# Delta heads: sums of squares as two rounded matmuls of a split square

## The reference, cut to what matters

```python
def l2norm(t):
    return t * lax.rsqrt(jnp.sum(t * t, axis=-1, keepdims=True) + 1e-6)

def gated_deltanet(h, w_in, conv_w, a_log, dt_bias, o_norm_g, w_out):
    qkv, gate, a_raw, b_raw = jnp.split(h @ w_in, ...)
    qkv = jax.nn.silu(causal_dwconv(qkv, conv_w)).astype(f32)
    q, k, v = jnp.split(qkv, [GDN_QK, 2 * GDN_QK], axis=-1)
    q = l2norm(q.reshape(bsz, L, GDN_HEADS, GDN_DK)) * (GDN_DK ** -0.5)
    k = l2norm(k.reshape(bsz, L, GDN_HEADS, GDN_DK))
    ...
    # triangular systems of each chunk, then the recurrence over chunks
    o = rmsnorm(o, o_norm_g) * jax.nn.silu(gate.astype(f32).reshape(...))
    return o.reshape(bsz, L, GDN_V).astype(h.dtype) @ w_out
```

## Time and profile before

| | us |
|---|---|
| median of 3 runs | 3143.57 |
| lowest and highest | 3140.71 and 3145.73 |
| the profiled execution | 3141.96 |
| its span, first to last instruction | 3140.2 |
| PE busy | 3054.4 (97%) |
| DVE busy | 1886.1 (60%) |
| ACT busy | 1110.5 (35%) |
| POOL busy | 598.6 (19%) |

### The profile page before, as it was taken

How to read it: one execution, slowest core, us unless ns; L and a number is a source line. 1 busy time by engine, 2 the same in 40 slices (tenths; PEclk the granted TensorE clock), 3 DMA queues, 4 the chain that set the end, 5 groups by cost and what they waited for, 6 DMA issues and landing times.

```text
span 3140.2 us, 41151 instructions
## 1 busy us (share of the span) xinstructions
PE 3054.4 (97%) x14594; PEld 2491.2 (79%) x14594; DVE 1886.1 (60%) x2257; ACT 1110.5 (35%) x1502; POOL 598.6 (19%) x1031
## 2 busy tenths in 40 slices
PE   8999999999999999998998899999999999989997
PEld 6888888878888888886886788888887788878886
DVE  6545454557677676776337455555555566666666
ACT  4111111245445454454134344444433222222223
POOL 1000000024444344443043222222202000000002
PEclk9999999999999999999999999999999999999998
DMA  3111111131111011114311211111121556597771
GB/s 102 54 42 53 41 53 43 45 101 34 47 33 53 27 53 47 33 47 138 110 48 36 91 37 37 37 37 37 37 76 54 177 192 231 191 362 243 245 245 70
DMA packets 336227, 285.48 MB, mean 91 GB/s; under 512 B 80776, under 2 KB 283528, under 8 KB 335888
## 3 DMA queue, kind: packets, MB, share of 16 engines
q1 hardware_dynamic: 336144, 284.38, 28.9%
HBM read 203.57 MB, written 80.77 MB: 91 GB/s over the span
## 4 chain that ended last, share of the span: by engine, by line
PE 91%; DVE 3%; issue 2%; ACT 1%; POOL 1%; DMA 1%; SPq 0%; DVEq 0%; POOLq 0%; ACTq 0%
PE banks L852 12%; PE banks L854 12%; PE banks L853 12%; PE banks L955 9%; PE banks L956 9%; PE banks L957 9%; PE banks L1355 3%; PE banks L1357 3%; PE banks L1356 3%; PE banks L985 2%; PE banks L1133 1%; PE banks L1215 1%; PE banks L1208 1%; PE banks L998 1%; PE banks L1000 1%
## 5 line engine op out<-in xcount | busy, mean ns | idle before, releaser
L955 PE MATMUL banks<-state_a_hi,weights_hi 128*128 128x512 f32 x1352 | 577.6, 427 | 1.1 <-DVE projection_staged L1941 1.1
L956 PE MATMUL banks<-state_a_lo,weights_hi 128*128 128x512 f32 x1352 | 534.0, 395 | 0.0
L957 PE MATMUL banks<-state_a_hi,weights_lo 128*128 128x512 f32 x1352 | 533.8, 395 | 0.0
L1392 ACT ACTIVATE weights_hi<-weights_raw 128x1024 fp32r<-128x1024 f32 x194 | 204.5, 1054 | 574.7 <-PE banks L854 489.7
L1798 DVE TENSOR_TENSOR weights_lo<-weights_raw,weights_hi 128x1024 fp32r<-128x1024 f32 x194 | 261.3, 1347 | 135.4 <-ACT weights_hi L1392 132.9
L957 PEld LDWEIGHTS banks<-state_a_hi,weights_lo 128*128 128x128 f32 x1352 | 254.3, 188 | 60.5
L955 PEld LDWEIGHTS banks<-state_a_hi,weights_hi 128*128 128x128 f32 x1352 | 256.1, 189 | 44.0 <-issue 2.6
L956 PEld LDWEIGHTS banks<-state_a_lo,weights_hi 128*128 128x128 f32 x1352 | 256.4, 190 | 39.2 <-issue 2.6
L1925 DVE TENSOR_TENSOR_SCAN stick_left<-stick_left,eps_column 128x128 f32<-128x128 f32 (+1 forms) x192 | 243.4, 1268 | 39.3 <-POOL beta L701 33.4
L852 PE MATMUL banks<-state_a_hi,weights_hi 128*128 128x512 f32 x648 | 256.7, 396 | 2.3 <-DVE stream_again L2177 1.5
L854 PE MATMUL banks<-state_a_hi,weights_lo 128*128 128x512 f32 x648 | 256.3, 395 | 0.0
(11 more groups left out here) (387 smaller groups left out, 5982.0 us busy)
## 6 DMA issues: line engine op xcount, KB each, us to landing
relu_blocks_dram<-relu_sums_staged SPq DMA_DIRECT2D x16, 2048.0 KB, 10.0
weights_raw<-in_mlp_w_dram SPq DMA_DIRECT2D x48, 512.0 KB, 5.1
relu_blocks_dram<-relu_blocks_staged SPq DMA_DIRECT2D x16, 1536.0 KB, 6.0
weights_raw<-in_gdn_w_in_dram SPq DMA_DIRECT2D x33, 512.0 KB, 4.1
weights_raw<-in_pool_w_in_dram SPq DMA_DIRECT2D x32, 512.0 KB, 3.8
weights_raw<-in_sb_w_in_dram SPq DMA_DIRECT2D x32, 512.0 KB, 4.2
relu_b<-relu_blocks_dram SPq DMA_DIRECT2D x16, 1024.0 KB, 10.7
state_b_hi<-relu_blocks_dram SPq DMA_DIRECT2D x16, 1024.0 KB, 14.3
```

Of the source, the lines that this page charges most:

```text
L955: pe.matmul(psum[:, bank, :], whi, hi, start=(k == 0), stop=False)
L956: pe.matmul(psum[:, bank, :], whi, lo, start=False, stop=False)
L957: last = pe.matmul(psum[:, bank, :], wlo, hi, start=False, stop=(k == end - 1))
L1392: act.activation(w_hi[slot][:, :], raw[slot][:, :], ACT.Copy).then_inc(weights_hi, 1)
```

## The change

Three pairs of tiles are added, all laid over tiles that are free at the time: `square_hi` (fp32r; for k and q over `oT`, for o over `XT`) and `square_lo` (over the squares themselves), and `mean_r`, an fp32r copy of `mean_of` that ACT makes once ahead of the heads.

- ACT: behind each of `sqk`, `sqq` and `osq` a second Square of the same source, written as fp32r (`khi`, `qhi`, `ohi`), 128x1024 each.
- DVE: a new subtraction `squares - hi` (`klo`, `qlo`, `olo`), 128x1024 each, at numbers 6, 18 and between `k_to_end` and `scores_decayed` (in the last head, behind `oT`).
- PE: a half of a sum was one fp32 matmul of 128x512 and is now two fp32r matmuls. They wait for the rest from DVE and no more for the square from ACT. The q sums move from 18 and 20 to 19 and 21, `normed_q` on DVE from 22 to 24, and in the last head `osums` from behind k = 3 to behind k = 5 of the output tile.
- Ahead of the heads: the first squares wait also for `pre_pe` and `g_saved`; `klo` stands on DVE behind `dl`, `qlo` behind `rescale(2, KC)`. At a full head's end DVE waits for its own `y2`.

```diff
         DVE_PREP = ["klo", "kn", "NT0", "NT1", "qlo", "qn", "kdec", "QD", "qd"]
...
-                ev.wait("act", f"{which}_ln0") if h else ev.wait("act", f"sq{which}")
-                ev.did(f"{which}_sum{h}", pe.matmul(psum[:, 7, :], mean_of[:, :], squares[:, 4 * h:4 * h + 4, :].rearrange("p c n -> p (c n)"), start=True, stop=True))
+                ev.wait("act", f"{which}_ln0") if h else ev.wait("dve", f"{which}lo")
+                hs = slice(h * HALF, h * HALF + HALF)
+                pe.matmul(psum[:, 7, :], mean_r[:, :], square_hi[which][:, hs], start=True, stop=False)
+                ev.did(f"{which}_sum{h}", pe.matmul(psum[:, 7, :], mean_r[:, :], square_lo[which][:, hs], start=False, stop=True))
...
-                            if h == 0 and k == 3:
+                            if h == 0 and k == 5:
                                 between()
...
-                        if n in (18, 20):
-                            norm_sum("q", (n - 18) // 2)
+                        if n in (19, 21):
+                            norm_sum("q", (n - 19) // 2)
...
-                    ev.wait("act", "osq")
+                    ev.wait("dve", "olo")
                     for h in range(2):
-                        last = pe.matmul(psum[:, 6 + h, :], mean_of[:, :], vn[:, 4 * h:4 * h + 4, :].rearrange("p c n -> p (c n)"), start=True, stop=True)
+                        hs = slice(h * HALF, h * HALF + HALF)
+                        pe.matmul(psum[:, 6 + h, :], mean_r[:, :], square_hi["o"][:, hs], start=True, stop=False)
+                        last = pe.matmul(psum[:, 6 + h, :], mean_r[:, :], square_lo["o"][:, hs], start=False, stop=True)
...
                 ev.did("sqq", act.activation(flat(qn), qT[:, :], ACT.Square))
+                ev.did("qhi", act.activation(square_hi["q"][:, :], qT[:, :], ACT.Square))
...
                 ev.did("sqk", act.activation(flat(k_next), kT[:, :], ACT.Square))
+                ev.did("khi", act.activation(square_hi["k"][:, :], kT[:, :], ACT.Square))
...
                 ev.did("osq", act.activation(vn[:, :, :], oT[:, :, :], ACT.Square))
+                ev.did("ohi", act.activation(square_hi["o"][:, :], flat(oT), ACT.Square))
...
+            act.activation(mean_r[:, :], mean_of[:, :], ACT.Copy).then_inc(mean_rounded, 1)
             silu(kT, True)
+            act.wait_ge(pre_pe, 1)
+            act.wait_ge(g_saved, 16)
             squares_k(1)
...
+            def square_rest(which):
+                squares = {"k": k_next, "q": qn, "o": vn}[which]
+                ev.wait("act", f"{which}hi")
+                ev.did(f"{which}lo", dve.tensor_tensor(square_lo[which][:, :], flat(squares), square_hi[which][:, :].bitcast(F32), ALU.subtract))
+            square_rest("k")
...
+                    if n == 6:
+                        square_rest("k")
+                    if n == 18:
+                        square_rest("q")
...
-                    if n == 22:
+                    if n == 24:
                         normed_q()
...
                     k_to_end(e + 1)
                     fill(n); n += 1
+                    square_rest("o")
                     scores_decayed()
...
-                if kind == "last":
-                    ev.wait("dve", "y2")
+                ev.wait("dve", "y2")
...
             rescale(2, KC)
+            square_rest("q")
             normed_q()
```

More of the change, by code:

```diff
@@ L180, in build @@
         kT, qT, qn, k_next = (place(n, [P, S]) for n in ("k_conv", "q_or_v_conv", "q_normed", "k_normed_next"))
+        square_q, square_k = qn, k_next
         qn, k_next = (x[:, :].rearrange("p (c n) -> p c n", n=P) for x in (qn, k_next))
@@ L206, in build @@
         last_row = place("last_row_ones", [P, P])
+        square_hi = {n: nc.alloc_sbuf_tensor_at(f"squares_hi_{n}", [P, S], F32R, offset=x.manual_sbuf_range[0]) for n, x in (("k", oT), ("o", XT))}
+        square_hi["q"] = square_hi["k"]
+        square_lo = {n: nc.alloc_sbuf_tensor_at(f"squares_lo_{n}", [P, S], F32R, offset=x.manual_sbuf_range[0]) for n, x in (("k", square_k), ("q", square_q), ("o", vn))}
+        mean_r = place("mean_matrix_rounded", [P, P], F32R)
         g_dram = nc.dram_tensor("log_decay_dram", (HEADS, S), F32).ap()
@@ L243, in build @@
         d_pe, d_dve, d_act = sem("delta_products"), sem("delta_vector"), sem("delta_scalar")
-        conv_done = sem("conv_done")
+        conv_done, mean_rounded = sem("conv_done"), sem("mean_rounded")
         pool_chunk, pool_squared, pool_summed, pool_mean = sem("pool_chunk_final"), sem("pool_squared"), sem("pool_summed"), sem("pool_mean")
@@ L266, in build @@
         PE_PREP = ["k_sum0", "k_sum1", "scores_k0", "scores_k1", "q_sum0", "q_sum1", "turn_k", "scores"]
-        DVE_PREP = ["kn", "NT0", "NT1", "qn", "kdec", "QD", "qd"]
-        ACT_PREP = ["sqk", "expD", "expG", "k_ln0", "k_ln1", "k_root", "sqq", "q_ln0", "q_ln1", "q_root"]
+        DVE_PREP = ["klo", "kn", "NT0", "NT1", "qlo", "qn", "kdec", "QD", "qd"]
+        ACT_PREP = ["sqk", "khi", "expD", "expG", "k_ln0", "k_ln1", "k_root", "sqq", "qhi", "q_ln0", "q_ln1", "q_root"]
         POOL_PREP = ["dsub", "maskD", "Db", "x0", "xb", "knc"]
@@ L272, in build @@
         DVE_MAIN = ([f"{x}{l}" for l in range(LEVEL0, LEVELS) for x in ("P1_", "X_")]
-                    + [f"{x}{c}" for c in range(TT) for x in ("R", "vw", "St") if (c or x != "R") and (c < TT - 1 or x != "St")] + ["oT", "y1", "y2"])
-        ACT_MAIN = ["XT3", "vn", "XT4", "XT5", "XT6", "osq", "oln", "ors"]
+                    + [f"{x}{c}" for c in range(TT) for x in ("R", "vw", "St") if (c or x != "R") and (c < TT - 1 or x != "St")] + ["oT", "olo", "y1", "y2"])
+        ACT_MAIN = ["XT3", "vn", "XT4", "XT5", "XT6", "osq", "ohi", "oln", "ors"]
         EVENTS = {("pe", 0): (d_pe, PE_MAIN), ("dve", 0): (d_dve, DVE_MAIN), ("act", 0): (d_act, ACT_MAIN),
@@ L1138, in norm_sum @@
             def norm_sum(which, h):
-                squares = (qn, k_next)["qk".index(which)]
                 if which == "q" and h == 0:
                     ev.wait("dve", "NT1")
-                ev.wait("act", f"{which}_ln0") if h else ev.wait("act", f"sq{which}")
-                ev.did(f"{which}_sum{h}", pe.matmul(psum[:, 7, :], mean_of[:, :], squares[:, 4 * h:4 * h + 4, :].rearrange("p c n -> p (c n)"), start=True, stop=True))
+                ev.wait("act", f"{which}_ln0") if h else ev.wait("dve", f"{which}lo")
+                hs = slice(h * HALF, h * HALF + HALF)
+                pe.matmul(psum[:, 7, :], mean_r[:, :], square_hi[which][:, hs], start=True, stop=False)
+                ev.did(f"{which}_sum{h}", pe.matmul(psum[:, 7, :], mean_r[:, :], square_lo[which][:, hs], start=False, stop=True))
             def scores_k(h):
@@ L1265, in _ @@
             v_silu = [0]
+            pe.wait_ge(mean_rounded, 1)
             for h in range(2):
@@ L2134, in _ @@
             did("dl", dve.tensor_tensor(kdec_s[:, :, :], glast[:, :, :], Gn[:, :, :], ALU.subtract))
+            ev = Events(dve, "dve")
+            flat = lambda x: x[:, :, :].rearrange("p c n -> p (c n)")
+            def square_rest(which):
[3 more added lines that the diff above has]
+            square_rest("k")
             dve.wait_ge(pre_act, PRA["eg"])
```

2 lines of the change are left out of this document (removed).

## The result

The changed kernel takes 3147.25 us (median of 20 runs), the kernel before 3141.62 us beside it (20 runs): a ratio of 1.0018 [1.0012, 1.0024]. It is slower by some 5.6 us. That is just inside the 0.2% that the prediction called no difference, but with 20 runs on each side the interval lies above 1: the loss is measurable. The profiled execution has a span of 3145.3 us against 3140.2.

The account below looks back on a forecast made before the run. PE was taken to bound the kernel (91% of the last chain); +0.8 in seven heads, +0.2 first, +0.6 last on 3141.96 gave 3143.6, raised by 1.6 towards the median to 3145 us, range 3134 to 3151.

Parts of the forecast that it names:

- The sum: Whole kernel: +0.8 us in seven full heads, +0.2 first head, +0.6 last head, on the profiled 3141.96: 3143.6.
- No measurable difference: Whole kernel: forecast 3145 us or no measurable difference, with about 0.2%, 6.3 us, as the least that can be told.
- What PE gains: PE's sums in a full head: four k and q halves at 0.39 plus output 0.79, 2.35 us gained.
- The k split: Full head, U0 on PE: ACT's added rounded square delays XT6, PE loses 0.97 us; the 0.9 at K2 stays.
- The q split: Full head, first q sum: PE waits 1.4 us for qlo, plus 0.1 for a matmul starting from a wait.
- The output split: Full head, output sums: olo ends before PE's slot, so it is hidden, with 0.7 us to spare.
- The new wait for `y2`: Full head's end on DVE, ahead of the next P1: some 0.2 us, covered on PE; taken as nothing, at most 0.2.
- The first head: First head: between -1.2 and +1.7 us from a later inverse chain against a possibly full clock; +0.2 taken.
- The last head: Last head: sums start two k steps later, the chain to state_a_lo ends 0.6 us later; bounds 0 and +1.5.
- Rival 1: Full heads: ACT and DVE have room, the gain stays; in part 3135 us, chance 0.10, in full 3128, 0.06.
- Rival 2: Full heads: POOL's inversion, slowed by DVE operations, becomes the last event; 3152 to 3162 us, chance 0.12.
- Rival 3: Mean sums on PE: a rounded matmul costs what the fp32 one did, only new work remains; 3162 us, chance 0.04.

Follow-up runs that it names:

- experiment 9: Changed kernel without the loop-end y2 wait, k and q rounding and sums reordered, last head's sums back behind k = 3: 3124.55 us, ratio 0.9946 to the kernel before.
- experiment 5: Kernel before with only the output split (rounded square, rest, four rounded matmuls): 3136.32 us, ratio 0.9985.
- experiment 3: Changed kernel with the rounded square of k behind XT6 on ACT, klo at number 7, k sums at 8 and 9: 3140.16 us, ratio 0.9999 to kernel before.
- experiment 1: Kernel before with one line of the change: DVE waits for its own y2 at every head's end: 3143.61 us, ratio 1.0012.
- experiment 2: Changed kernel without the loop-end y2 wait; ACT waits for a later DVE step instead: 3142.76 us, ratio 1.0007 to the kernel before.
- experiment 4: Changed kernel with ACT rounding the weight tile ahead of the rounded square of q at number 18: 3141.05 us, ratio 0.9998 to the kernel before.

## Why the prediction held, and where it was off

Forecast were 3145 us, in a range of 3134 to 3151; measured 3147.25. The sum said +1.6 us and it was 5.6, so the change is off by 4.0 and not by 2.25. The other 1.8 are luck: the forecast was counted up from a median of 3 runs, 3143.57, and the median of 20 is 3141.62. "No measurable difference" was wrong as well. Of the 4.0, 2.3 are the new wait for `y2`, and about 1.5 the clock in the last head. Term by term:

- **What PE gains, 2.35 a head.** Right, 2.37 (experiment 9); the output's part 0.74 for 0.79 (experiment 5).
- **The k split, 0.97 a head.** Right, 0.97 (experiment 3); the wait at U0 is in all seven heads, and the wait at K2 stayed at 0.9 as was said. XT6 starts 1.92 after the square of k, where 1.94 was forecast.
- **The q split, 1.4 + 0.1.** Right in kind, 1.19 of idle time. I stacked DVE's two operations at 1.22 each; they start 1.14 apart. That lies at the low bound that I had given (1.2). By subtraction, 80.24 - 77.43 - 0.97 - 0.43, the q split costs 1.41 a head in all, against 1.5 forecast; 0.2 of it come on top of the idle time, where 0.1 was forecast.
- **The output split, hidden.** Right: `olo` is there when PE comes.
- **The new wait for `y2`, "I take nothing, and at most 0.2".** This is the step that failed. It costs 0.47 and 0.43 a head (experiments 1 and 2) in heads 1 to 5 and 0.1 in head 6, 2.3 us in all. I priced the wait as the end of one DVE operation. But it stands at the end of the loop's body: the next head's first instruction can start 0.52 after `y2` ends and not 0.1 before. Where the same wait has no turn of the loop behind it, ahead of the last head, P1 follows at 1.32:

```profile
2299.93 1.28 DVE L2300 SCALAR_TENSOR_TENSOR delta_mixed<-o_T,o_norm_gain,delta_gate 128x1024 f32<-128x1024 f32 x1
2301.25 0.69 DVE L2253 TENSOR_TENSOR inverse_step<-banks,level_masks 128x512 f32<-128x512 f32 x1
```

  1.32 against 1.20 without a wait and 1.81 in the loop: so 0.12 is the wait and 0.49 the turn, which otherwise runs while DVE is still busy. The trace has what fills the turn. In the head of the rows above (`y2` from 1899.35) the loop's branch starts at 1900.75, the next instruction of the loop at 1901.04 and P1 at 1901.16; at the entry to head 6, where the branch doesn't jump back, P1 starts 0.10 after the branch. So 0.3 of the turn is the jump back. In the kernel before the branch of that turn starts at 1898.30, under `y2`. And PE's cover, transposes and two triples, which I took to be enough, was short by 0.33 where I had not laid the times side by side.
- **The first head, +0.2.** It came out at about 0, from two shifts in opposite directions as laid out: in the profiled execution its preparation took 1.2 us longer from the first k sum to the first product, and its solution 1.2 less. The waits were 9.82 (forecast some 10) and 3.4 (3 to 5). The wait before the second half of the first k sum, 0.78 before, is 2.13, which was not forecast; PE waits for the blocks later in any case.
- **The last head, +0.6.** The chain through the sums is 2386.30 - 2372.33 = 13.97 us from the output's square to the wait's end, before 13.37: +0.60, right. But the head is 2.1 longer in the profiled execution. The other 1.5 come ahead of that square, and I had not counted them at all. They fit the clock: 42 us at 0.80 for 0.84, an estimate of 42 x 0.04 = 1.7. Experiments 1 and 5 have the same clock of 0.80 and the same 1.5 ahead of the square, without the k and q splits.
- **Rival 1, the gain stays:** fell, both waits are there, and both can be taken away (experiments 3, 4, 9). **Rival 2, POOL as the last event:** fell, PE waits for the blocks once, in the first head. **Rival 3, no cheaper matmul:** fell, they are 0.23 apart.

What stays open is why the last head's clock differs. Experiment 1 differs from the kernel before by the wait alone, and its window from 2298 has 0.80; experiment 2 lacks the wait and has 0.88. That would fit, but the output sums alone (no such wait) have 0.80 too, the kernel with XT6 first (with the wait) has 0.84, and the one with the rest ahead of the rescalings 0.67:

```profile
2300.00:2342.00 42.00, 36.83 (x188) 33.54 (x187) 18.34 (x22) 16.65 (x17) 0.00 (x0) 0.67 0.34 101
```

Those 0.67 explain the 91.93 us of its last head. But these are one execution a kernel, and that last one is the slowest of its 11 runs. Shown is only that two executions of the kernel before agree, and three of the changed one; whether 0.67 and 0.88 belong to their kernels is not shown, and no edit here sets the clock on purpose.

## What to carry to other kernels

Cheaper matmuls bring their gain only if the work that pays for them stands behind, and not ahead of, whatever PE is about to wait for on the other engines; here two swaps in ACT's order, one step each, gave back 1.9 us a head, and with the remainders and sums a number later and the wait at the loop's end gone a loss became the whole gain, with the engines' loads nearly unchanged. A wait at the end of a loop's body costs its own time and the loop's turn as well, so it should be asked of a later reader, on another engine if need be. And an edit is best priced with its neighbours' distances from start to start rather than with durations.

## What the runs showed of the hardware

- **The clock differs in a stretch with the same work.** The last head's 42 us, with 36.7 to 36.8 of them busy, ran at a mean granted clock of 0.67 to 0.88 over thirteen executions of ten kernels, with 0.84 in both of the kernel before and 0.80 in all three of the changed one; the execution with 0.67 was some 4 us longer there than those with 0.80. The first head's clock is looser: 0.72 and 0.52 in two executions of the same kernel, with 1.6 us between them.
- **Consecutive ACT and DVE operations overlap:** a 128x1024 fp32 activation lasts 1.06 us and the next starts after 0.95 to 0.97; a subtraction of that size lasts 1.22 and the next starts after 1.14 (1868.65 to 1869.79).
- **A loop's turn on DVE costs 0.49 us where nothing runs over it.** From the branch that jumps back to the next instruction it is 0.29 us (1900.75 to 1901.04), from the one at the entry to head 6, which doesn't, 0.10. Under a running operation of DVE (branch at 1898.30, before) the turn costs nothing: 1.20 from `y2` to P1 in the loop.
- **A POOL step of the inversion takes 1.02 us while DVE subtracts one SBUF tile from another, and 0.26 right after.** In the first head of the changed kernel, `qlo` ends at 1713.93:

```profile
1713.03 1.02 POOL L802 TENSOR_TENSOR inverse_blocks<-inverse_blocks,inverse_blocks_outer 64x36 f32<-64x36 f32 x1 [0.18 <-POOL inverse_blocks_outer L798]
1714.22 0.26 POOL L798 TENSOR_TENSOR inverse_blocks_outer<-inverse_blocks 64x44 f32<-64x44 f32 x1 [0.18 <-POOL inverse_blocks L802]
```

  The first of them ends 0.1 after `qlo` does. The new remainder held back one POOL step there, by some 0.75 us. In each full head it meets one as well (0.87 to 0.91 us), and PE noticed none of these.

  The Trainium skill, "SBUF — State Buffer", section "SBUF: two separate sides", says that of a DVE instruction with two SBUF inputs and a GpSimd instruction that reads SBUF the first to start holds the port pair they share for the whole instruction, and the other is blocked. What this trace shows agrees for the step from 1713.03: it lasts until `qlo` is done.
